# The residual kept in the output tensors, and the last sum made by accumulating DMAs: one layer of a retention / convolution / expert model on one core

## Chip, cores and metric
The kernel runs on one core of a Trainium2 chip. The metric is the device time of one execution in microseconds (us); lower is better. Everything is computed in fp32.

## The reference, cut to what matters
One layer is applied to 128 context tokens (x_prompt) and 1024 latent tokens (x_sample), width 1024. For each group of tokens:

```python
h = rmsnorm(x, n_pre_mix) * (1.0 + sc1) + sh1
m, s_f, s_b = mixer(h, ...)                 # retention and short convolution, then @ w_o
x = x + g1 * rmsnorm(m, n_post_mix)         # the residual, called x1 below
h = rmsnorm(x, n_pre_ffn) * (1.0 + sc2) + sh2
f = expert_choice_ffn(h, ...)               # 16 experts, each takes its best 128 + 16 tokens
x = x + g2 * rmsnorm(f, n_post_ffn)         # the output
```

`rmsnorm(f, g)` is `f * rsqrt(mean(f*f) + 1e-6) * g`. The expert outputs of one token, from however many experts chose it, are summed into f. The outputs are the new x of both groups and the two final retention states of the context.

## The kernel before, in words
The 1152 tokens are nine tiles of 128 rows: tile 0 is the context, tiles 1 to 8 are the latent tokens. The program gives each engine its own list of instructions; semaphores order them. Nothing is scheduled by a tool: what stands first in an engine's list is issued first, and a wait holds all that stands behind it on that engine.

- **Up to about 1290 us**: modulation, input projection, retention and convolution, with TensorE on weights that are split in a high and a low part (L743 to L745).
- **Mixing, about 1290 to 1410 us**: for each tile, TensorE multiplies by w_o. DVE makes x1 from the product, the gate and the tile of x (L1674, L1679), and then the experts' input h2 (L1687, L1689). ACT squares and sums for the two norms (L1226, L1232). POOL turns each sum into a reciprocal root by `rstd` (L580 to L584: an add, a wait for it, a pow), and stores x1 (L633) and h2 (L638) to the scratch tensors x1_d and h2_d in DRAM. `store(t, b)` does this for tile t and buffer b; it runs in a loop of four passes with two tiles each, and once more for tile 8 (L640 to L643).
- **Routing, to about 1480 us**: the experts' tokens are chosen; ffn_d, the sum of the expert outputs in DRAM, is filled with zeros by nine stores of POOL (L650).
- **Experts, to 2298 us**: for each of 16 experts POOL gathers its rows of h2 by an indirect DMA, TensorE multiplies by the three weights (L976), DVE scales the result (L1797, L1799), and POOL adds its 128 and 16 rows into ffn_d by two indirect accumulating DMAs (L673, L675). SP loads the weights. Once the fifth unit of the last expert is made, SP also loads all nine tiles of x1 from x1_d to x1_all (L559).
- **The last part**, which the change rewrites. SP waits until all rows are added, then loads f in three groups of three tiles (f_all, L563). ACT squares and sums the nine tiles in order (L1303, `f_sq`). For each group, POOL multiplies the third tile by g2 (already holding the gate times n_post_ffn; L683), then makes `rstd` of the group's three sums (L582, L584). DVE multiplies the first two tiles by g2 (L1810), waits for the group's `rstd`, and computes y = (f * g2) * rstd + x1 for three tiles (L1816). SP stores each tile of y to the outputs as it becomes ready (L567), and waits for all stores.

Queues: DMAs issued by SP and ACT go through the hardware queue (q1 in the profile), those of POOL through the software queue (q0). All use the same 16 DMA engines.

The tail of DVE before:

```python
for g in range(3):
    dve.wait_ge(f_in_s[g], 16)
    for t in (3 * g, 3 * g + 1):
        did(dve.tensor_tensor(y_all[:, t, :], f_all[:, t, :], g2[:, min(t, 1), :], ALU.mult))
    settle()
    dve.wait_ge(f_rstd, g + 1)
    for t in range(3 * g, 3 * g + 3):
        if t % 3 == 2:
            dve.wait_ge(f_scaled, g + 1)
        dve.scalar_tensor_tensor(y_all[:, t, :], y_all[:, t, :], f_rs[:, t:t + 1], x1_all[:, t, :], ALU.mult, ALU.add)
```

Of the kernel before, what the change touches and what calls it, by code (L numbers as in the profile page):

```python
# [6 lines left out]
ALU = mybir.AluOpType  # L7
# [6 lines left out]
P = 128  # L14
D = 1024
# [3 lines left out]
NT = TOK // P  # L19
# [5 lines left out]
EXPERTS = 16  # L25
# [100 lines left out]
class Steps:  # L126
# [5 lines left out]
    def did(self, ins):  # L132
        ins.then_inc(self.sem, 1)
        self.n += 1

    def settle(self):
        self.eng.wait_ge(self.sem, self.base + self.n)
# [23 lines left out]
def build(nc, x_prompt, x_sample, state_f, state_b, c, c_ctx, w_ada, b_ada, n_pre_mix, n_post_mix,  # L161
          n_pre_ffn, n_post_ffn, w_in, dec_f, dec_b, gn_g, conv_w, w_ret_o, w_conv_o, w_o, w_router,
          w_gate, w_up, w_down, small_tab, rope_tab, y_prompt, y_sample, new_f, new_b):
    with ExitStack() as ctx:
        BASE = 16512

        def at(name, offset, shape, dt=F32):
            return nc.alloc_sbuf_tensor_at(name, shape, dt, offset=BASE + offset)

        def sem(name):  # L170
            return ctx.enter_context(nc.semaphore(name))

        def dram(name, shape):
            return nc.dram_tensor(name, shape, F32, kind="Internal").ap()
# [49 lines left out]
        f_ms, f_rs = x_ms, x_rstd  # L224
# [58 lines left out]
        x1 = [at(f"x1_{j}", Z + (14 + j) * SL, [P, D]) for j in range(2)]  # L283
# [32 lines left out]
        g2 = at("g2", Z + 9 * SL, [P, 2, D])  # L316
        norm_ffn = at("norm_ffn", Z + 17 * SL, [P, D])
        sq3 = at("sq3", Z + 16 * SL, [P, D])
        x1_all = at("x1_all", 0, [P, NT, D])
        f_all = at("f_all", 10 * SL, [P, NT, D])  # L320
        y_all = at("y_all", Z, [P, NT, D])

# [8 lines left out]

        mod_d = dram("mod_d", [2, 4 * D])
        merged_d = dram("merged_d", [KD, P, TOK])
        x1_d = dram("x1_d", [NT, P, D])
        h2_d = dram("h2_d", [TOK, D])
        ffn_d = dram("ffn_d", [TOK, D])

# [52 lines left out]
        xg_turned, xT_ready, out_turned, out_ready = sem("xg_turned"), sem("xT_ready"), sem("out_turned"), sem("out_ready")  # L390
        added_l, added_c = sem("added_l"), sem("added_c")
        g2_in = sem("g2_in")
        x1_landed = sem("x1_landed")
        f_in_s = [sem(f"f_in_s{g}") for g in range(3)]
        f_sq, f_rstd, f_scaled = sem("f_sq"), sem("f_rstd"), sem("f_scaled")
        y_ready, y_stored = sem("y_ready"), sem("y_stored")
        m_rstd, x1_rstd, gn_var, gn_rstd = sem("m_rstd"), sem("x1_rstd"), sem("gn_var"), sem("gn_rstd")

        tally = {}
# [14 lines left out]
        def _(sp):  # L414
# [140 lines left out]
                    load_unit(e, j, False)  # L555


            sp.wait_ge(unit_made, 12 * (EXPERTS - 1) + 5)
            sp.dma_start(x1_all[:], x1_d.rearrange("t p d -> p t d")).then_inc(x1_landed, 16)  # L559
            sp.wait_ge(added_l, 16 * EXPERTS)  # L560
            sp.wait_ge(added_c, 16 * EXPERTS)
            for g in range(3):
                sp.dma_start(f_all[:, 3 * g:3 * g + 3, :], ffn_d[3 * g * P:(3 * g + 3) * P, :].rearrange("(t p) d -> p t d", p=P))\  # L563
                  .then_inc(f_in_s[g], 16)
            for t in range(NT):
                sp.wait_ge(y_ready, t + 1)
                sp.dma_start(ys[t - 1] if t else yp, y_all[:, t, :]).then_inc(y_stored, 16)  # L567
            sp.wait_ge(y_stored, 16 * NT)


        @block.gpsimd
        def _(pool):
# [7 lines left out]
            def rstd(dst, src, eps):  # L580

                pool_steps.did(pool.tensor_tensor(dst, src, eps, ALU.add))  # L582
                pool_steps.settle()
                return pool.tensor_tensor(dst, dst, minus_half[:, 0:dst.shape[-1]], ALU.pow)  # L584
# [40 lines left out]
                pool.dma_start(merged_d[n], merged[:]).then_inc(merged_stored, 16)  # L625


            def store(t, b):
                pool.wait_ge(m_sq, t + 1)
                rstd(stats[:, 8 + b:9 + b], stats[:, 4 + b:5 + b], rms_eps[:, 0:1]).then_inc(m_rstd, 1)  # L630
                pool.wait_ge(x1_ready, t + 1)
                plain(pool)
                pool.dma_start(x1_d[bass.ds(t, 1)].rearrange("a p d -> (a p) d"), x1[b][:]).then_inc(x1_stored[b], 16)  # L633
                pool.wait_ge(x1_sq, t + 1)
                rstd(stats[:, 12 + b:13 + b], stats[:, 6 + b:7 + b], rms_eps[:, 0:1]).then_inc(x1_rstd, 1)
                pool.wait_ge(h2_ready, t + 1)
                plain(pool)
                pool.dma_start(h2_d[bass.ds(t * P, P), :], h2[b][:]).then_inc(h2_stored[b], 16)  # L638

            with pool_steps.loop(4, 4) as i:  # L640
                store(2 * i, 0)
                store(2 * i + 1, 1)
            store(8, 0)  # L643

            pool.wait_ge(logit_made, NT)
# [30 lines left out]
                                        compute_op=ALU.add).then_inc(added_c, 16)  # L676


            pool.wait_ge(g2_ready, 2)
            for g in range(3):  # L680
                ts, t = slice(3 * g, 3 * g + 3), 3 * g + 2
                pool.wait_ge(f_in_s[g], 16)
                pool.tensor_tensor(y_all[:, t, :], f_all[:, t, :], g2[:, 1, :], ALU.mult).then_inc(f_scaled, 1)  # L683
                pool.wait_ge(f_sq, 3 * g + 3)
                rstd(f_rs[:, ts], f_ms[:, ts], rms_eps[:, ts]).then_inc(f_rstd, 1)
            pool.wait_ge(state_stored, 32 * HEADS)


# [618 lines left out]
        def _(dve):  # L1307
# [495 lines left out]


            dve.wait_ge(g2_ready, 2)
            dve.wait_ge(x1_landed, 16)
            for g in range(3):
                dve.wait_ge(f_in_s[g], 16)
                for t in (3 * g, 3 * g + 1):
                    did(dve.tensor_tensor(y_all[:, t, :], f_all[:, t, :], g2[:, min(t, 1), :], ALU.mult))  # L1810
                settle()
                dve.wait_ge(f_rstd, g + 1)
                for t in range(3 * g, 3 * g + 3):
                    if t % 3 == 2:
                        dve.wait_ge(f_scaled, g + 1)
                    dve.scalar_tensor_tensor(y_all[:, t, :], y_all[:, t, :], f_rs[:, t:t + 1], x1_all[:, t, :], ALU.mult, ALU.add)\  # L1816
                       .then_inc(y_ready, 1)


# [26 lines left out]
```

## Time and profile before

| what | value |
|---|---|
| median of three runs | 2342.23 us (2341.36 to 2344.58) |
| span of the profiled execution, first to last instruction | 2342.5 us |
| granted TensorE clock, mean | 0.965 of full speed (2.4 GHz) |
| busy: PE / PEld / DVE / ACT / POOL | 2148.6 / 2036.2 / 707.5 / 372.5 / 183.2 us |
| DMA | 357.37 MB, mean 153 GB/s |
| end of the last transposes on PE | 2297.7 us |
| last operation on DVE starts | 2338.0 us |

The profiled execution is known by its span of 2342.54 us, the first instruction's start to the last one's end; it is 0.3 us over the median of the runs.

How to read it: PE is TensorE's matmuls, PEld its weight loads, DVE VectorE, ACT ScalarE, POOL GpSimd, SP the engine that only issues DMAs. L12 is line 12 of the kernel; a helper's line is named for all that it issues. Buffer numbers and digits are left out of names, so x_d is x1_d, x_all is x1_all, h_d is h2_d. Times are us from the start of the span. In a line of the timeline the columns are start, duration, engine, line, operation, output<-inputs with shapes, count, and in brackets the idle time ahead of it with what ended it. A DMA line with "GB/s" gives the rate in 40 equal slices of its window; under it each queue has its packets, MB and the time of its packets as a share of 16 engines' window.

### The profile page before, as it was taken

The page shows a single profiled execution, that of the slowest core. Times are in us where ns is not written, and L with a number is a line of the kernel's source. Part 1 is how long each engine was busy: PE and PEld are TensorE (multiplying, and loading weights), DVE is VectorE, ACT ScalarE, POOL GpSimd, SP SyncE. Part 2 cuts the span into 40 slices and gives each one's busy share as a digit, 9 for nine tenths or more (in the row PEclk, how much of TensorE's full clock was granted, in tenths as well). Part 3 has the DMA queues.
Part 4 walks back from the last instruction along what each step waited for, and adds up shares of the span by engine and source line. Part 5 has one row for each costly group of instructions (what it writes and reads, how often), then busy time and mean ns, then how long its engine had stood idle before and what let it go on. Part 6 is the DMA issues. An engine that isn't in the chain of part 4 may idle for free.

```text
span 2342.5 us, 34417 instructions
## 1 busy us (share of the span) xinstructions
PE 2148.6 (92%) x14065; PEld 2036.2 (87%) x14065; DVE 707.5 (30%) x1203; ACT 372.5 (16%) x586; POOL 183.2 (8%) x245
## 2 busy tenths in 40 slices
PE   5899999997999999999999892899999999999992
PEld 1689898987999999999999781899999999999992
DVE  1634343446655323232123547001000000100004
ACT  4421212122111121111112330100000000000001
POOL 1000000000000000000000211001100000110003
PEclk9999999999999999999999995899999999999996
DMA  8101010101444211112225638588888888888854
GB/s 280 29 27 38 20 37 19 37 19 55 134 142 137 81 45 36 52 37 75 85 76 201 216 127 305 191 269 254 273 277 277 270 262 268 253 272 279 277 197 172
DMA packets 329939, 357.37 MB, mean 153 GB/s; under 512 B 9924, under 2 KB 297612, under 8 KB 329764
## 3 DMA queue, kind: packets, MB, share of 16 engines
q1 hardware_dynamic: 315760, 308.41, 41.5%
q0 software_dynamic: 14032, 48.29, 6.9%
q8 instruction: 32, 0.52, 0.1%
q14 instruction: 15, 0.12, 0.0%
q10 hardware_dynamic: 100, 0.03, 0.0%
HBM read 318.39 MB, written 38.31 MB: 152 GB/s over the span
## 4 chain that ended last, share of the span: by engine, by line
PE 85%; issue 5%; DVE 5%; DMA 2%; ACT 1%; POOL 1%; ACTq 0%; DVEq 0%; SPq 0%; POOLq 0%
PE ps L976 32%; PE ps L743 13%; PE ps L745 13%; PE ps L744 13%; PE ps L900 1%; PE ps L902 1%; PE ps L901 1%; PE ps L778 1%; DMA xa<-in_x_sample_dram 1%; PE ps L1004 1%; PE ps L917 1%; PE ps L792 1%; PE ps L784 1%; PE ps L966 1%; PE ps L1006 1%
## 5 line engine op out<-in xcount | busy, mean ns | idle before, releaser
L743 PE MATMUL ps<-h_hi,w_hi 128*128 128x384 f32 x1536 | 524.2, 341 | 10.9 <-DVE h_lo L1372 8.7
L744 PE MATMUL ps<-h_lo,w_hi 128*128 128x384 f32 x1536 | 515.6, 336 | 0.0
L745 PE MATMUL ps<-h_hi,w_lo 128*128 128x384 f32 x1536 | 515.3, 336 | 0.0
L976 PE MATMUL ps<-xT,wq 128*128 128x144 f32 x4096 | 506.3, 287 | 1.3 <-ACT xT L1276 1.3
L976 PEld LDWEIGHTS ps<-xT,wq 128*128 128x128 f32 x4096 | 504.5, 191 | 1.7 <-ACT xT L1276 1.4
L743 PEld LDWEIGHTS ps<-h_hi,w_hi 128*128 128x128 f32 x1536 | 290.2, 189 | 25.2 <-issue 12.5
L744 PEld LDWEIGHTS ps<-h_lo,w_hi 128*128 128x128 f32 x1536 | 290.2, 189 | 1.9 <-issue 1.9
L745 PEld LDWEIGHTS ps<-h_hi,w_lo 128*128 128x128 f32 x1536 | 289.9, 189 | 0.0
L976 PE MATMUL ps<-hid,wq 128*128 128x144 f32 x2048 | 255.1, 287 | 0.7 <-issue 0.7
L976 PEld LDWEIGHTS ps<-hid,wq 128*128 128x128 f32 x2048 | 251.7, 190 | 1.3 <-issue 0.9
L1378 DVE TENSOR_TENSOR w_lo<-w_raw,w_hi 128x1024 fp32r<-128x1024 f32 x80 | 97.6, 1220 | 227.2 <-ACT w_hi L1063 226.6
L1791 DVE TENSOR_TENSOR hid<-ps,sg 128x288 f32<-128x288 f32 x64 | 29.3, 458 | 450.5 <-PE ps L976 450.5
L743 PE MATMUL ps<-z_hi,w_hi 128*128 128x384 f32 x384 | 128.5, 335 | 0.0
L745 PE MATMUL ps<-z_hi,w_lo 128*128 128x384 f32 x384 | 128.4, 334 | 0.0
L744 PE MATMUL ps<-z_lo,w_hi 128*128 128x384 f32 x384 | 128.4, 334 | 0.0
L1797 DVE TENSOR_SCALAR ot_l<-ps,val_l 128x1024 f32<-128x1024 f32 x16 | 20.5, 1284 | 312.4 <-PE ps L1006 312.4
L1063 ACT CAST w_hi<-w_raw 128x1024 fp32r<-128x1024 f32 x80 | 83.9, 1049 | 160.6 <-PE ps L745 86.1
L1285 ACT ACTIVATE sg<-ps 128x288 f32<-128x288 f32 x64 | 26.2, 410 | 453.2 <-PE ps L976 453.2
L1563 DVE SCALAR_TENSOR_TENSOR ada_acc<-ada_k,cond,ada_acc 128x512 f32<-128x512 f32 x112 | 79.2, 749 | 41.6 <-DMA ada_k<-in_w_ada_dram 40.2
L673 POOL DMA_INDIRECT ffn_d<-ot_l,idx_l x16 | 25.8, 1612 | 738.9 <-DVE ot_c L1799 738.9
L743 PEld LDWEIGHTS ps<-z_hi,w_hi 128*128 128x128 f32 x384 | 72.1, 188 | 0.2 <-issue 0.2
L744 PEld LDWEIGHTS ps<-z_lo,w_hi 128*128 128x128 f32 x384 | 72.1, 188 | 0.0
(227 smaller groups left out, 1786.1 us busy)
## 6 DMA issues: line engine op xcount, KB each, us to landing
wq<-in_w_down_dram SPq DMA_DIRECT2D x64, 1024.0 KB, 5.4
wq<-in_w_gate_dram SPq DMA_DIRECT2D x64, 1024.0 KB, 7.1
wq<-in_w_up_dram SPq DMA_DIRECT2D x64, 1024.0 KB, 7.1
w_raw<-in_w_in_dram SPq DMA_DIRECT2D x64, 512.0 KB, 4.1
ada_k<-in_w_ada_dram SPq DMA_DIRECT2D x64, 256.0 KB, 2.8
merged_d<-merged POOLq DMA_DIRECT2D x16, 576.0 KB, 3.5
ada<-in_w_ada_dram SPq DMA_DIRECT2D x4, 2048.0 KB, 14.4
ret_part<-merged_d POOLq DMA_DIRECT2D x8, 576.0 KB, 4.2
```

The source lines that it names most:

```text
L673: pool.indirect_dma_start(ffn_d, bass.IndirectOffsetOnAxis(ap=idx_l[:, e:e + 1], axis=0), ot_l[:], None, compute_op=ALU.add).then_inc(adde ...
L743: pe.matmul(out, w_hi[:, slot, k, :], xh, start=(k == 0), stop=False)
L744: pe.matmul(out, w_hi[:, slot, k, :], xl, start=False, stop=False)
L745: mm = pe.matmul(out, w_lo[:, slot, k, :], xh, start=False, stop=(k == KD - 1))
L778: return pe.matmul(bank(b, 512), lhsT, src[:, 1 + 4 * x:5 + 4 * x, :], start=True, stop=True)
L784: mm = pe.transpose(ps[:, b, s * P:(s + 1) * P], src[:, t, :], ident)
L976: mm = pe.matmul(ps[:, j % 4, m * CAP:(m + 1) * CAP], wq[j][:, k, m * P:(m + 1) * P], src[:, k, :], start=(k == 0), stop=(k == KD - 1))
L1063: act.copy(w_hi[:, c_ % 2], w_raw[:, c_ % 2]).then_inc(w_hi_done, 1)
L1285: act.activation(sg[:], unit_of(2 * q), ACT.Silu).then_inc(unit_act, 1)
L1378: dve.tensor_tensor(w_lo[:, c_ % 2], w_raw[:, c_ % 2], w_hi[:, c_ % 2].bitcast(F32), ALU.subtract)\
L1563: ins = dve.scalar_tensor_tensor(ada_acc[:, w_, :], ada_k[k % 2][:], cond[:, k, w_:w_ + 1], ada_acc[:, w_, :], ALU.mult, ALU.add)
L1791: dve.tensor_tensor(hid[:, 2 * q:2 * q + 2, :], ps[:, (2 * q + 1) % 4, 0:2 * CAP].rearrange("p (m n) -> p m n", m=2), sg[:], ALU.mult)\
```

## The change
x1 is no longer stored to a scratch tensor: POOL's stores in the mixing part write it straight to the outputs (tile 0 to y_prompt, the others to y_sample), and it is not read back. In the last part DVE makes one operation for each tile, y_all = (f * rstd) * g2, and POOL issues an accumulating DMA for each tile that adds y_all to the x1 that lies in the output. The multiplies on POOL and the first multiplies on DVE go. POOL's order in the last part is: rstd 1, rstd 2, adds of group 1, rstd 3, adds of group 2, adds of group 3. POOL's store loop has its first pass written out ahead of the loop, since tile 0 goes to another tensor. The whole diff:

```diff
@@ -316,7 +316,6 @@
         g2 = at("g2", Z + 9 * SL, [P, 2, D])
         norm_ffn = at("norm_ffn", Z + 17 * SL, [P, D])
         sq3 = at("sq3", Z + 16 * SL, [P, D])
-        x1_all = at("x1_all", 0, [P, NT, D])
         f_all = at("f_all", 10 * SL, [P, NT, D])
         y_all = at("y_all", Z, [P, NT, D])
 
@@ -331,7 +330,6 @@
 
         mod_d = dram("mod_d", [2, 4 * D])
         merged_d = dram("merged_d", [KD, P, TOK])
-        x1_d = dram("x1_d", [NT, P, D])
         h2_d = dram("h2_d", [TOK, D])
         ffn_d = dram("ffn_d", [TOK, D])
 
@@ -390,10 +388,9 @@
         xg_turned, xT_ready, out_turned, out_ready = sem("xg_turned"), sem("xT_ready"), sem("out_turned"), sem("out_ready")
         added_l, added_c = sem("added_l"), sem("added_c")
         g2_in = sem("g2_in")
-        x1_landed = sem("x1_landed")
         f_in_s = [sem(f"f_in_s{g}") for g in range(3)]
-        f_sq, f_rstd, f_scaled = sem("f_sq"), sem("f_rstd"), sem("f_scaled")
-        y_ready, y_stored = sem("y_ready"), sem("y_stored")
+        f_sq, f_rstd = sem("f_sq"), sem("f_rstd")
+        y_ready, y_added = sem("y_ready"), sem("y_added")
         m_rstd, x1_rstd, gn_var, gn_rstd = sem("m_rstd"), sem("x1_rstd"), sem("gn_var"), sem("gn_rstd")
 
         tally = {}
@@ -555,17 +552,12 @@
                     load_unit(e, j, False)
 
 
-            sp.wait_ge(unit_made, 12 * (EXPERTS - 1) + 5)
-            sp.dma_start(x1_all[:], x1_d.rearrange("t p d -> p t d")).then_inc(x1_landed, 16)
             sp.wait_ge(added_l, 16 * EXPERTS)
             sp.wait_ge(added_c, 16 * EXPERTS)
             for g in range(3):
                 sp.dma_start(f_all[:, 3 * g:3 * g + 3, :], ffn_d[3 * g * P:(3 * g + 3) * P, :].rearrange("(t p) d -> p t d", p=P))\
                   .then_inc(f_in_s[g], 16)
-            for t in range(NT):
-                sp.wait_ge(y_ready, t + 1)
-                sp.dma_start(ys[t - 1] if t else yp, y_all[:, t, :]).then_inc(y_stored, 16)
-            sp.wait_ge(y_stored, 16 * NT)
+            sp.wait_ge(y_added, 16 * NT)
 
 
         @block.gpsimd
@@ -625,21 +617,29 @@
                 pool.dma_start(merged_d[n], merged[:]).then_inc(merged_stored, 16)
 
 
+            def add_to_output(g):
+                for t in range(3 * g, 3 * g + 3):
+                    pool.wait_ge(y_ready, t + 1)
+                    pool.dma_start(ys[t - 1] if t else yp, y_all[:, t, :], accum_op=ALU.add).then_inc(y_added, 16)
+
             def store(t, b):
+
                 pool.wait_ge(m_sq, t + 1)
                 rstd(stats[:, 8 + b:9 + b], stats[:, 4 + b:5 + b], rms_eps[:, 0:1]).then_inc(m_rstd, 1)
                 pool.wait_ge(x1_ready, t + 1)
                 plain(pool)
-                pool.dma_start(x1_d[bass.ds(t, 1)].rearrange("a p d -> (a p) d"), x1[b][:]).then_inc(x1_stored[b], 16)
+                dst = yp if isinstance(t, int) and t == 0 else ys[bass.ds(t - 1, 1)].rearrange("a p d -> (a p) d")
+                pool.dma_start(dst, x1[b][:]).then_inc(x1_stored[b], 16)
                 pool.wait_ge(x1_sq, t + 1)
                 rstd(stats[:, 12 + b:13 + b], stats[:, 6 + b:7 + b], rms_eps[:, 0:1]).then_inc(x1_rstd, 1)
                 pool.wait_ge(h2_ready, t + 1)
                 plain(pool)
                 pool.dma_start(h2_d[bass.ds(t * P, P), :], h2[b][:]).then_inc(h2_stored[b], 16)
 
-            with pool_steps.loop(4, 4) as i:
+            def two_stores(i):
                 store(2 * i, 0)
                 store(2 * i + 1, 1)
+            pool_steps.each(4, 4, two_stores)
             store(8, 0)
 
             pool.wait_ge(logit_made, NT)
@@ -676,13 +676,13 @@
                                         compute_op=ALU.add).then_inc(added_c, 16)
 
 
-            pool.wait_ge(g2_ready, 2)
             for g in range(3):
-                ts, t = slice(3 * g, 3 * g + 3), 3 * g + 2
-                pool.wait_ge(f_in_s[g], 16)
-                pool.tensor_tensor(y_all[:, t, :], f_all[:, t, :], g2[:, 1, :], ALU.mult).then_inc(f_scaled, 1)
+                ts = slice(3 * g, 3 * g + 3)
                 pool.wait_ge(f_sq, 3 * g + 3)
                 rstd(f_rs[:, ts], f_ms[:, ts], rms_eps[:, ts]).then_inc(f_rstd, 1)
+                if g:
+                    add_to_output(g - 1)
+            add_to_output(2)
             pool.wait_ge(state_stored, 32 * HEADS)
 
 
@@ -1803,18 +1803,10 @@
 
 
             dve.wait_ge(g2_ready, 2)
-            dve.wait_ge(x1_landed, 16)
-            for g in range(3):
-                dve.wait_ge(f_in_s[g], 16)
-                for t in (3 * g, 3 * g + 1):
-                    did(dve.tensor_tensor(y_all[:, t, :], f_all[:, t, :], g2[:, min(t, 1), :], ALU.mult))
-                settle()
-                dve.wait_ge(f_rstd, g + 1)
-                for t in range(3 * g, 3 * g + 3):
-                    if t % 3 == 2:
-                        dve.wait_ge(f_scaled, g + 1)
-                    dve.scalar_tensor_tensor(y_all[:, t, :], y_all[:, t, :], f_rs[:, t:t + 1], x1_all[:, t, :], ALU.mult, ALU.add)\
-                       .then_inc(y_ready, 1)
+            for t in range(NT):
+                dve.wait_ge(f_rstd, t // 3 + 1)
+                dve.scalar_tensor_tensor(y_all[:, t, :], f_all[:, t, :], f_rs[:, t:t + 1], g2[:, min(t, 1), :], ALU.mult, ALU.mult)\
+                   .then_inc(y_ready, 1)
 
 
 # ---- launch: one core; inputs and outputs as the reference has them ----
```

## Rows read from the trace of the kernel before
**Rows 1.** The page, part 4: the chain that ended last, by engine.
```profile
PE 85%; issue 5%; DVE 5%; DMA 2%; ACT 1%; POOL 1%; ACTq 0%; DVEq 0%; SPq 0%; POOLq 0%
```

**Rows 2.** Busy time by stretch (columns: us; PE, PEld, DVE, ACT, POOL busy; PEclk, DMA share, GB/s).
```profile
1560.00:2290.00 730.00, 721.43 (x5923) 713.43 (x5922) 60.58 (x85) 62.57 (x142) 65.96 (x54) 1.00 0.84 261
...
2290.00:2345.00 55.00, 7.21 (x59) 6.57 (x58) 26.70 (x17) 11.14 (x20) 18.95 (x11) 0.62 0.51 182
```

**Rows 3.** Chain that ended last, in order of time, from 2290 us.
```profile
2302.63 4.65 DMA ffn_d<-ot_c,idx_c
...
2307.35 6.38 DMA f_all<-ffn_d
...
2319.52 5.26 DVE y_all L1816 x3
...
2325.12 4.50 DVE y_all L1810 x2
...
2335.63 1.28 DVE y_all L1816
```

**Rows 4.** Timeline of ACT and POOL in the last part.
```profile
2317.47 0.96 POOL L582 TENSOR_TENSOR stats<-stats,small 128x3 f32<-128x3 f32 x1 [0.17 <-ACT sq L1303]
...
2318.51 0.89 POOL L584 TENSOR_TENSOR stats<-stats,small 128x3 f32<-128x3 f32 x1
...
2321.21 0.19 ACT L1303 ACTIVATION_READ_ACCUMULATOR sq<-f_all 128x1 f32 x1
...
2321.69 1.17 POOL L582 TENSOR_TENSOR stats<-stats,small 128x3 f32<-128x3 f32 x1
...
2322.95 1.77 POOL L584 TENSOR_TENSOR stats<-stats,small 128x3 f32<-128x3 f32 x1
...
2324.93 0.19 ACT L1303 ACTIVATION_READ_ACCUMULATOR sq<-f_all 128x1 f32 x1
```

**Rows 5.** Instructions on the tile y_all (min/median/max ns, first and last start).
```profile
L1816 DVE SCALAR_TENSOR_TENSOR y_all<-y_all,stats,x_all x9: 1271/1280/3289, 2319.5 to 2338.0; 128x1024 f32<-128x1024 f32 x9
...
L567 SPq DMA_DIRECT2D out_dram<-y_all x9: 332/332/356, 2322.8 to 2339.3; - x9
```

**Rows 6.** Traffic of the last scatter-add: 2302 to 2307, 2304.5 to 2306, 2305 to 2305.5, 2300 to 2308.
```profile
GB/s 0 0 0 0 0 0 0 426 98 0 0 66 131 33 98 66 229 66 131 197 229 131 229 164 229 229 197 229 164 229 262 164 164 230 164 66 98 0 0 0
...
q0 software_dynamic: 77, 0.31, 102.8%
...
2305.00:2305.50 0.50, 0.00 (x0) 0.00 (x0) 0.00 (x0) 0.00 (x0) 0.00 (x0) 0.50 1.11 221
...
q0 software_dynamic: 176, 0.59, 48.0%
```

**Rows 7.** The two operations of `rstd` elsewhere (tiles stats and gnr, whole span).
```profile
L582 POOL TENSOR_TENSOR stats<-stats,small x22: 179/194/1176, 41.4 to 2327.4; 128x1 f32<-128x1 f32 x18, 128x3 f32<-128x3 f32 x3, 128x9 f32<-128x9 f32 x1
...
L584 POOL TENSOR_TENSOR gnr<-gnr,small x24: 565/1007/1024, 160.8 to 548.5; 128x4 f32<-128x4 f32 x16, 128x1 f32<-128x1 f32 x8
```

**Rows 8.** POOL's DMA issues: timeline, traffic from 1395.5 to 1401.5, tile ffn_d.
```profile
1290.69 1.45 POOL L584 TENSOR_TENSOR stats<-stats,small 128x1 f32<-128x1 f32 x1
...
1396.17 0.60 POOL L633 DMA_DIRECT2D x_d<-x  x1 [3.61 <-DVE x L1679]
...
GB/s 0 0 0 0 0 0 0 0 0 0 109 0 328 410 355 410 410 355 410 410 273 28 27 27 27 27 0 0 0 0 0 0 0 0 0 0 0 0 0 0
...
x_d<-x POOLq DMA_DIRECT2D x1, 512.0 KB, 3.8
...
1423.78 0.53 POOL L650 DMA_DIRECT2D ffn_d<-zero  x1 [0.37 <-issue]
...
L673 POOL DMA_INDIRECT ffn_d<-ot_l,idx_l x16: 1589/1611/1630, 1532.8 to 2300.7; - x16
```

**Rows 9.** Traffic from 2322.5 to 2345 us, in 40 slices.
```profile
GB/s 0 0 379 415 393 408 386 422 393 0 0 0 0 0 0 0 218 415 386 408 408 408 415 138 0 0 0 357 415 386 415 401 408 408 7 0 0 0 0 0
```

**Rows 10.** Busy time while x1 is read back, same columns as rows 2.
```profile
2269.00:2279.00 10.00, 9.64 (x79) 9.43 (x77) 0.69 (x2) 0.41 (x1) 0.00 (x0) 1.00 1.02 409
```

## The prediction
> **What bounds the kernel now.** The chain that ended last comes first: TensorE carries 85% of the span [rows 1]. Busy time by stretch then shows that the change lies almost wholly outside that part. In the expert stage (1560 to 2290 us) PE is busy 721 of 730 us, while in the last 55 us it has 7 us of work and what the other engines and the DMA do is the span [rows 2]. The chain in order of time gives the links of that end: the last scatter-add lands at 2307.28, the first third of f_all at 2313.73, and from 2319.52 the chain is DVE alone, alternating between L1816 and L1810 until the last y tile [rows 3]. The last store is issued at 2339.3 [rows 5], and the span ends at 2342.54. The traffic from 2322.5 on shows three bursts of about 400 GB/s with empty slices between them, so now the stores wait for DVE and not DVE for the stores [rows 9]. ACT is not late: its ninth square is done at 2325.12, 14 us before the last store [rows 4].
>
> **Removed from the path.** DVE loses six multiplies (the two on the chain at 2325.12 cost 4.50 us) and POOL its three, which shared the time with DVE: L1816 takes 1.28 us in the median and 3.29 at worst [rows 3, 5]. What is left for DVE is nine operations of 1.28 us, 11.5 us instead of the 19.8 from 2319.52 to 2339.3. Read alone, this promises some 8 us. It is not the forecast, because the transfers change kind.
>
> **Added: nine adds to DRAM.** No direct accumulating DMA is in this trace; the nearest rows are the scatter-add of expert 15, 144 rows of 4 KB from SBUF added into DRAM, which ran with no other traffic. From 2304.5 to 2306, in its steady part, 77 packets passed with the 16 queues busy to 102.8%: 16 x 1.5 / 77 = 0.312 us for a 4 KB packet on one DMA engine, 205 GB/s [rows 6]. A plain store or load runs at 400 to 415 GB/s [rows 8, 9], so an added row costs twice a stored one. The change adds 9 x 128 = 1152 rows, 72 for each of the 16 engines: 72 x 0.312 = **22.4 us**. One end of the bound is the best half microsecond, 221 GB/s [rows 6]: 4.72 MB / 221 = 21.4 us. A lower end is the plain rate, 408 GB/s [rows 9]: 11.6 us. The upper end is the mean packet of the whole scatter-add, its slow start included: 48.0% of 16 x 8 us over 144 packets is 0.427 us [rows 6], and 72 of them take 30.7 us. I take 0.312, since 1152 packets in a row are much nearer to the steady part than to the start; the direct form has the same 4 KB rows and adds in the same DMA engines.
>
> The start costs extra once. All 144 rows, 9 for an engine, went from 2302.87 to about 2306.6 [rows 6], 3.7 us where 9 x 0.312 is 2.8: **0.9 us**.
>
> **When the stream can begin.** The third square ends at 2317.4 and POOL starts `rstd` at 2317.47 as now [rows 4]. Its first operation took 0.96 us beside DVE's multiply; with DVE idle such an operation takes 0.18 to 0.19 [rows 4, 7]. The second took 0.89 with DVE mostly idle, between the 0.57 and 1.01 of one and four columns elsewhere [rows 4, 7]. So rstd 1 is done at 2317.47 + 0.20 + 0.08 + 0.89 = 2318.65, not 2319.40. DVE makes y 0 to 2 from 2318.75 to 2318.75 + 3 x 1.28 = 2322.6. The sixth square is done at 2321.40 [rows 4]. POOL's add then runs beside DVE (1.17 us as now), to 2322.6, and its pow mostly without it (0.89): rstd 2 at 2323.6. Bounds: 0.2 for the first gives 2322.6, and 1.77 for the second, as now, 2324.5 [rows 4]. Only after rstd 2 does POOL come to the first add, although y 0 has been ready since 2320.0: three ready tiles stand behind a wait for a later group's squares. A direct store on POOL shows its first bytes 0.83 us after its start (1396.17, traffic from 1397.0) [rows 8]. First packet: 2323.65 + 0.83 = **2324.5**.
>
> **Can POOL and DVE feed it?** One direct issue takes 0.53 us and comes every 0.90 [rows 8]; even at the 1.61 + 0.30 us of a scatter-add [rows 8] it is below the 8 x 0.312 = 2.50 us that one tile's add occupies the DMA engines. Tiles 3 to 5 are ready by 2327.5 (DVE from 2323.7), when the first three adds run until 2332.9. rstd 3 stands behind the three issues, 2323.65 + 3 x 0.90 = 2326.35, and is done by 2327.5 to 2329.4; y 8 by 2333.3 at worst, when the queue still holds adds until 2347. The queue never runs empty, so DVE's 8 us and every delay of rstd 3 cost and give nothing.
>
> **The sum.** 2324.5 + 0.9 + 22.4 = 2347.8 for the last byte. What follows the last byte is read from the end of the span before: the traffic stops at about 2341.65, the start of its last slice with a trace of it [rows 9], and the span ends 0.9 us later, landing and SP's last wait included; the scatter-add's last byte came 0.7 us ahead of its landing [rows 3, 6], which gives no other size. 2347.8 + 0.9 = 2348.7, against the span of 2342.54 +6.2. The median of the three runs is 2342.23, 0.3 below that span, so the forecast is **2348.4 us**.
>
> **Edits at nothing.** The x1 stores go to the outputs instead of a scratch tensor: same queue, place, bytes. The read of x1_all goes (4.6 MB at 409 GB/s), one issue on SP: PE was busy 9.64 of 10 us meanwhile [rows 10], so it covers the load, and at most 0.4 us comes back; SP has nothing else to issue until the last scatter-add lands at 2307.28 [rows 3]. The peeled first pass of POOL's loop: code met for the first time cost at most 1.45 - 0.57 = 0.9 us at 1290.69 [rows 7, 8], and a second copy of the body could cost that again, where `rstd` holds DVE. The removed waits for g2 on POOL and x1 on DVE were long fulfilled. I carry these as -0.4 to +0.9.
>
> **Rules weighed.** Traffic to DRAM reaches 415 GB/s here [rows 9], in both directions of this last part. The Trainium skill, DMA: Bandwidth & Descriptors, section Specifications, gives one core some 358 GB/s of HBM; an add both reads and writes its destination there, 9.4 MB, which by an estimate from that figure takes 26.4 us and ends the kernel at 2352.4. The trace does not agree for plain traffic, and its add moves 2 x 205 GB/s there.
>
> **Rivals.** (a) *The add runs at the plain rate*, the half rate of the scatter-add being due to its indirect rows. Then the stream is 11.6 us: 2324.5 + 11.6 + 0.9 = 2337.0. The producers allow about as much: rstd 3 at 2327.5 to 2329.4, three tiles of DVE more (y 8 at 2331.4 to 2333.3), then 0.83 + 1.3 (0.52 MB at 408 GB/s) + 0.9, 2336.3 at worst. As a time **2336.7**, faster than before. The point from which it decides: the time of before is kept where 72 packets take 2342.54 - 2324.5 - 1.8 = 16.2 us, 0.23 us for each; below that the change gains. For it: all accumulating rows of this trace are indirect. Against: their rate is steady across the burst and half the plain one, as if each row were read twice. The Trainium skill, DMA: Bandwidth & Descriptors, section Anatomy of one DMA, fits a POOL-issued DMA as 2.0 us plus its bytes over 436 GB/s, with no surcharge for adding; by it the stream would be 10.8 us, which is this rival. The 205 GB/s measured speak against it [rows 6].
> (b) *Plain rate, but POOL pays for an accumulating issue as for a scatter-add*, 1.61 + 0.30 us: nine issues and one `rstd` in a row, 2323.65 + 17.2 + 1.2 = 2342.0, then 0.3 + 1.3 + 0.9: 2344.5, as a time **2344.2**, within the bound of no change. For it: POOL would be the only engine that still works. Against: the direct stores' 0.53 us [rows 8].
> (c) *The adds don't overlap*: each pays the start again, 0.9 + 2.5 = 3.4 us, nine take 30.6 instead of 23.3: **2355.7**. The mean packet above gives nearly the same (30.7). Against: the three stores of a group run without a gap [rows 9], though those come from the other queue.
>
> **How the numbers follow.** A measurement of this kernel can tell about 0.2% from no change, 4.7 us: over 2346.9 is slower, under 2337.5 faster. The forecast's case has 0.77, the others 0.10 (a), 0.05 (b) and 0.08 (c). Within the forecast's case the earliest start (-1.0), the best rate (-1.0), a start cost of nothing (-0.9) and x1_all's 0.4 reach 2345.1; I give 0.15 to its part under 2346.9 and 0.62 above. So slower 0.70, same 0.20, faster 0.10. The range leaves out (a) and half of (b): 2344.5 to 2356.0.
>
> **What would show it.** In the profile after: first bytes of the last traffic near 2324.5; then one unbroken stretch at about 205 GB/s for 22 to 23 us, not three bursts; POOL's nine issues done by about 2334; DVE's nine operations at 1.28 us each, over by 2333; the chain's last link a DMA into the output. The prediction is wrong if that traffic passes 300 GB/s, if it has gaps (then the feeding, not the rate, is the bound), or if PE's last matmul ends over 1 us away from 2297.7, since that would be an effect of the edits ahead of the last part.

## The result, and the profile after

The changed kernel takes **2355.04 us** in the median of four runs (2353.13 to 2356.89), the kernel before 2343.29 in its four (2341.36 to 2344.58): slower by 0.51%, ratio 1.0051 with a 95% interval of 1.0036 to 1.0065. The forecast was 2348.4 with a range to 2356.0: the sign is right and the value inside, but the forecast had only 6.2 of the 11.75 us.

The page of the changed kernel, its first part and its queues:

```profile
span 2355.2 us, 34387 instructions
...
PE 2149.1 (91%) x14065; PEld 2036.6 (86%) x14065; DVE 694.5 (29%) x1197; ACT 372.5 (16%) x586; POOL 178.5 (8%) x251
...
q1 hardware_dynamic: 313296, 298.97, 40.2%
q0 software_dynamic: 15328, 53.01, 7.9%
```

PE did the same work in the same time. The 4.7 MB that q1 wrote as y now pass through q0 (53.01 MB, not 48.29), and q1 has lost another 4.7 MB, x1's way back. The loss is not ahead of the last part: PE's last transposes start at 2297.06, 0.4 us later than before, and in the other kernels below, with the same work up to there, they start between 2294.4 and 2297.2.

The timeline of the last part, POOL and DVE of the changed kernel (beside [rows 4, 5]):

```profile
2317.82 0.19 POOL L574 TENSOR_TENSOR stats<-stats,small 128x3 f32<-128x3 f32 x1 [13.47 <-ACT sq L1303]
2318.09 0.89 POOL L576 TENSOR_TENSOR stats<-stats,small 128x3 f32<-128x3 f32 x1
...
2319.10 3.68 DVE L1808 SCALAR_TENSOR_TENSOR y_all<-f_all,stats,g 128x1024 f32<-128x1024 f32 x3 [18.25 <-POOL stats L576]
...
2321.83 1.00 POOL L574 TENSOR_TENSOR stats<-stats,small 128x3 f32<-128x3 f32 x1 [2.85 <-ACT sq L1303]
...
2322.91 0.86 POOL L576 TENSOR_TENSOR stats<-stats,small 128x3 f32<-128x3 f32 x1
...
2323.72 2.75 POOL L623 DMA_DIRECT2D out_dram<-y_all  x3
2323.80 3.68 DVE L1808 SCALAR_TENSOR_TENSOR y_all<-f_all,stats,g 128x1024 f32<-128x1024 f32 x3 [1.02 <-POOL stats L576]
...
2325.63 1.88 POOL L574 TENSOR_TENSOR stats<-stats,small 128x3 f32<-128x3 f32 x1
2327.60 0.88 POOL L576 TENSOR_TENSOR stats<-stats,small 128x3 f32<-128x3 f32 x1
2328.45 5.25 POOL L623 DMA_DIRECT2D out_dram<-y_all  x6
2328.51 3.68 DVE L1808 SCALAR_TENSOR_TENSOR y_all<-f_all,stats,g 128x1024 f32<-128x1024 f32 x3 [1.04 <-POOL stats L576]
```

DVE makes its nine operations in three groups of 3.68 us and is done at 2332.2; before, it was done at 2339.3. The first add is issued at 2323.72, six issues in a row end at 2333.70. Then no instruction computes for 21 us. What happens in them is seen in the traffic from 2322 to 2352, in 40 slices of 0.75 us:

```profile
GB/s 0 0 0 0 87 126 208 180 202 169 202 197 197 213 218 202 213 213 197 208 218 202 213 213 208 213 213 218 202 202 218 213 213 208 208 87 11 0 0 0
...
q0 software_dynamic: 1296, 4.72, 82.9%
```

This is one unbroken stream from the slice at 2325.0 to about 2349.5, at 205 GB/s in the mean from 2326 to 2348 (slices of 197 to 218), where before there were three bursts of 400 [rows 9]. The packets took 82.9% of 16 x 30 us; over 1152 rows of 4 KB that is 0.345 us a row. And the traffic ends almost 6 us ahead of the span. The queue of SP's waits and the instructions that close the program (line, engine's sequencer, operation: duration in ns, start) tell what lies there:

```profile
SPq L164 <- DMA out_dram<-y_all: 40.9, 1, 40.9
SPq L164 <- PEq L164: 4.8, 1, 4.8
```

```profile
L164 POOLq EVENT_SEMAPHORE  x2: 17/17/17, 2355.0 to 2355.1; - x2
...
L164 POOLq COMPARE_BRANCH  x1: 41/41/41, 2332.7 to 2332.7; - x1
L164 POOLq DRAIN  x1: 22086/22086/22086, 2332.9 to 2332.9; - x1
L164 SPq COMPARE_BRANCH  x1: 38/38/38, 2350.2 to 2350.2; - x1
```

SP has its last landing at 2350.2 and then waits 4.8 us more (the name PEq is that of an engine in the closing meeting, not of the late one). The late one is POOL: behind its last instruction stands a DRAIN, which holds until 2355.0. In the trace of before, DVE's DRAIN ends with DVE's last operation, at 2339.3, and ACT's with ACT's, at 2325.1; POOL's does not. A DRAIN is taken up while the operation ahead of it still runs, so its end is what counts here, not its own duration. POOL's last operation and the same two lines in the kernel before:

```profile
2328.61 1.71 POOL L584 TENSOR_TENSOR stats<-stats,small 128x3 f32<-128x3 f32 x1
...
L164 POOLq DRAIN  x1: 11718/11718/11718, 2328.7 to 2328.7; - x1
...
L164 SPq COMPARE_BRANCH  x1: 38/38/38, 2342.2 to 2342.2; - x1
```

There the DRAIN ended at 2340.4, 10.1 us behind POOL's last operation (2328.61 + 1.71 = 2330.32) and 33 us behind the last landing of a DMA of POOL, and DVE's work hid it by 2 us. It is in no busy time and on no chain of the page.

### The profile page after: what moved, and what is told of

The parts are those of the page before. It is cut to its first block, busy times and chain, and to the rows that moved or that the text cites. A ratio compares the mean times of both kernels' runs of the same rounds, so it can differ in the third digit from the quotient of the medians.

```text
span 2355.2 us, 34387 instructions
## 1 busy us (share of the span) xinstructions
PE 2149.1 (91%) x14065; PEld 2036.6 (86%) x14065; DVE 694.5 (29%) x1197; ACT 372.5 (16%) x586; POOL 178.5 (8%) x251
## 3 DMA queue, kind: packets, MB, share of 16 engines
q0 software_dynamic: 15328, 53.01, 7.9%
## 4 chain that ended last, share of the span: by engine, by line
PE 84%; issue 5%; DVE 4%; DMA 2%; POOL 1%; ACT 1%; ACTq 0%; DVEq 0%; SPq 0%; POOLq 0%
PE ps L976 32%; PE ps L743 13%; PE ps L745 13%; PE ps L744 13%; PE ps L900 1%; PE ps L902 1%; PE ps L901 1%; PE ps L778 1%; DMA xa<-in_x_sample_dram 1%; PE ps L1004 1%; PE ps L917 1%; PE ps L792 1%; PE ps L784 1%; PE ps L966 1%; PE ps L1006 1%
## 5 line engine op out<-in xcount | busy, mean ns | idle before, releaser
L745 PEld LDWEIGHTS ps<-z_hi,w_lo 128*128 128x128 f32 x384 | 72.1, 188 | 0.0
```

The source lines that it names most:

```text
L745: mm = pe.matmul(out, w_lo[:, slot, k, :], xh, start=False, stop=(k == KD - 1))
```

## The experiments

Theory A at their start is in two parts: an adding row costs twice a plain one, which is a property of adding, not of POOL's queue (the software queue, q0); and POOL's closing DRAIN takes some 10 us from POOL's last work, of which the last 4.8 us come only after its last DMA has landed. Each time stands beside runs of the kernel before on the same chip; "end" is the end of the profiled span, and SP's COMPARE_BRANCH in the lines below marks the last landing that SP waits for.

### Plain stores from POOL's queue

```diff
-pool.dma_start(ys[t - 1] if t else yp, y_all[:, t, :], accum_op=ALU.add).then_inc(y_added, 16)
+pool.dma_start(ys[t - 1] if t else yp, y_all[:, t, :]).then_inc(y_added, 16)
```

> The changed kernel with the accumulation taken out of the nine last DMAs, which now overwrite the output: the addition of x1 is left out. Same queue, same issuing engine, same bytes written. Theory A (the adding doubles the time of a packet on the DMA engines, and POOL's closing DRAIN ends some 4.8 us after the last landing): packets of about 0.16 us, so the last traffic is bound by the producers and ends near 2335 to 2338, at about 400 GB/s in bursts; the span ends 4.8 us after the last landing or 10 us after POOL's last issue, about 2343 to 2345, some 11 us under the changed kernel. Rival B (the software queue, not the adding, sets the half rate): the stream stays at about 205 GB/s and the span near 2355.

Measured: 2344.07 us, ratio 1.0002 (0.9992 to 1.0011). The traffic of that run from 2320 to 2360, its last issue and its closing:

```profile
GB/s 422 123 0 0 0 344 336 406 393 274 344 385 401 393 397 393 397 254 0 0 0 0 0 0 0 0 0 0 0 0 0 0 0 0 0 0 0 0 0 0
...
q0 software_dynamic: 1296, 4.72, 30.3%
```

```profile
2332.44 0.53 POOL L623 DMA_DIRECT2D out_dram<-y_all  x1 [0.67 <-DVE y_all L1808]
```

```profile
L164 POOLq DRAIN  x1: 10357/10357/10357, 2332.6 to 2332.6; - x1
L164 SPq COMPARE_BRANCH  x1: 38/38/38, 2338.2 to 2338.2; - x1
```

The same 1296 packets through the same queue take 30.3% of 16 x 40 us, 0.168 us for each row of 4 KB, at up to 400 GB/s. So **adding doubles the row, the queue does not**. The second reading matters as much: even with the rows at the plain rate the kernel is no faster than before. DVE is done at 2332.1, the last row lands at 2338.2, but the last issue of POOL ends at 2332.97 and its DRAIN at 2343.0, 10.0 us later. That is also 4.8 us behind the last landing, so this run alone doesn't tell which of the two parts of A held the DRAIN.

### POOL waits for the adds

```diff
             pool.wait_ge(state_stored, 32 * HEADS)
+            pool.wait_ge(y_added, 16 * NT)
```

> The changed kernel, where POOL also waits for all nine adds before its list ends, so that its closing DRAIN starts only after the last landing at about 2350.2. Theory A (the DRAIN has a length of its own, about 10 us from POOL's last work, and runs beside the adds; in the changed kernel it is then held by the open DMAs): it now starts at 2350.2 and the span ends near 2360, 5 us later. Theory B (the DRAIN is only held by open software-queue DMAs and ends 4.8 us after the last landing whenever it starts): the span stays within 1 us of 2355. Theory C (with nothing open it returns at once): the span ends near 2351, 4 us earlier.

Measured: 2358.02 us (2357.56 to 2360.09), ratio 1.0066 (1.0049 to 1.0083), 3.0 us over the changed kernel's median.

```profile
L164 SPq COMPARE_BRANCH  x1: 38/38/38, 2346.5 to 2346.5; - x1
...
L164 POOLq DRAIN  x1: 8929/8929/8929, 2346.7 to 2346.7; - x1
```

With nothing open the DRAIN takes 8.9 us by itself. Theory B wanted the end 4.8 us behind the last landing, theory C right behind it. The profiled span, 2355.9, would by itself fit B, but PE's last transposes start 2.6 us earlier in this execution, and the closing lines put the end 9.1 us behind the landing. A holds; its 10 us were 1 too many here, and the extra time was 3.0 instead of 5 us, since the adds were also in about 1 us sooner, counted from the last scatter-add. In the changed kernel only 4.8 us lie behind the landing, so some 4 us of the DRAIN's time seem to run beside the adds.

### POOL waits for the stores in the kernel before

```diff
             pool.wait_ge(state_stored, 32 * HEADS)
+            pool.wait_ge(y_stored, 16 * NT)
```

> The kernel before, where POOL also waits for the nine stores of y (issued by SP) before its list ends. No DMA of POOL is open in this part, the last landed at 2307.3. Theory A (the DRAIN has about 10 us of its own, which the kernel before hides behind DVE's work): it starts near 2342.2 and the span ends at about 2352, 10 us over before. Theory B (the DRAIN follows only open software-queue DMAs): it ends at once and the span stays at 2342.5.

Measured: 2352.75 us, ratio 1.0041 (1.0026 to 1.0055), 9.7 us over the kernel before.

```profile
L164 SPq COMPARE_BRANCH  x1: 38/38/38, 2340.6 to 2340.6; - x1
...
L164 POOLq DRAIN  x1: 10113/10113/10113, 2340.8 to 2340.8; - x1
```

One wait that costs nothing by itself makes the kernel before nearly as slow as the changed one. No DMA of POOL was open. The DRAIN is 10.1 us long and counts from POOL's last instruction, here a wait.

### x1 in the outputs, and nothing else

```diff
-pool.dma_start(x1_d[bass.ds(t, 1)].rearrange("a p d -> (a p) d"), x1[b][:]).then_inc(x1_stored[b], 16)
+dst = yp if isinstance(t, int) and t == 0 else ys[bass.ds(t - 1, 1)].rearrange("a p d -> (a p) d")
+pool.dma_start(dst, x1[b][:]).then_inc(x1_stored[b], 16)
...
-sp.dma_start(x1_all[:], x1_d.rearrange("t p d -> p t d")).then_inc(x1_landed, 16)
+sp.dma_start(x1_all[:, 0, :], yp).then_inc(x1_landed, 16)
+sp.dma_start(x1_all[:, 1:NT, :], ys.rearrange("t p d -> p t d")).then_inc(x1_landed, 16)
```

The first pass of POOL's store loop is written out too, as in the change.

> One part of the change alone on the kernel before: x1 is stored straight into the outputs (with the first pass of the loop written out), is read back from there, and the last part stays as before. Theory A (this part costs nothing): within 1 us of before, the last transposes on PE end within 0.5 us of 2297.7. Rival (storing into the outputs or the longer code of POOL costs something): 1 to 3 us more, visible already in the mixing stage, 1290 to 1410 us.

Measured: 2341.72 us, ratio 0.9997 (0.9987 to 1.0006): no difference, as expected of the time. PE's last transposes start at 2294.97 and end 1.7 us earlier than in the profile of before; the expected 0.5 us was too narrow, since this point moves by 2.8 us from kernel to kernel (2294.4 to 2297.2), and nothing got later. So these edits cost nothing that can be measured, and all of the loss is in the last part.

### The adds ahead of the next rstd

```diff
                 rstd(f_rs[:, ts], f_ms[:, ts], rms_eps[:, ts]).then_inc(f_rstd, 1)
-                if g:
-                    add_to_output(g - 1)
-            add_to_output(2)
+                add_to_output(g)
```

> The changed kernel with POOL's order in the last part turned: the adds of a group stand right behind its rstd, ahead of the next rstd. Theory A (the end is the stream of adds plus a fixed 4.8 us of DRAIN behind the last landing): the first add is issued at about 2320.5 instead of 2323.7, the stream of 22.5 us and the end move up by the same 3 us, span near 2352, though rstd 2 and 3 and DVE come later. Rival (POOL's last issue decides, which moves only if DVE does): the last issue stays near 2333 and the span within 1 us of 2355.

Measured: 2352.42 us (2349.11 to 2353.92), ratio 1.0039 (1.0024 to 1.0055), 2.6 us under the changed kernel's median.

```profile
2318.64 0.98 POOL L623 DMA_DIRECT2D out_dram<-y_all  x1 [1.71 <-DVE y_all L1806]
...
2333.57 0.86 POOL L623 DMA_DIRECT2D out_dram<-y_all  x1 [0.56 <-DVE y_all L1806]
```

```profile
L164 POOLq DRAIN  x1: 17002/17002/17002, 2333.7 to 2333.7; - x1
L164 SPq COMPARE_BRANCH  x1: 38/38/38, 2345.9 to 2345.9; - x1
```

The last issue is no earlier than in the changed kernel, though f's load was 2.2 us earlier; the first one is 5.1 us earlier, 2.9 us beyond that shift. The last landing (2345.9) is 4.3 us earlier, 2.1 beyond the shift, and the end once more lies 4.8 us behind it (2350.8). The rival, that the last issue decides, falls: POOL's last issue ends at 2334.4, 16 us ahead of the end. It is the stream that sets the end, plus 4.8 us. Theory A had put 3 us on it and 2.6 were measured in the medians, though the ranges of the two kernels touch (2353.13 is the changed kernel's lowest).

### DVE's saving alone

```diff
-                if g:
-                    add_to_output(g - 1)
-            add_to_output(2)
...
+            for t in range(NT):
+                sp.wait_ge(y_ready, t + 1)
+                sp.dma_start(ys[t - 1] if t else yp, y_all[:, t, :]).then_inc(y_added, 16)
             sp.wait_ge(y_added, 16 * NT)
```

> DVE's saving alone: the changed kernel, where SP stores the nine tiles of y with plain DMAs (the addition of x1 is left out) and POOL ends with rstd 3. Theory A (POOL's DRAIN takes 10 us from its last work): DVE is done at 2332.2 and the last store would be in by 2335.3, but POOL's last work ends near 2327.5 to 2328.5 and the DRAIN at about 2338: span near 2338, 4 to 5 us under before, where the one-operation tile alone would give 7. Rival (the DRAIN costs nothing if no DMA of POOL is open): span near 2335.5, 7 us under before. Against the plain stores issued by POOL (span 2343.2) it tells what moving the last issue to POOL costs: 5 us.

Measured: 2338.69 us, ratio 0.9985 (0.9975 to 0.9994).

```profile
2326.08 1.77 POOL L579 TENSOR_TENSOR stats<-stats,small 128x3 f32<-128x3 f32 x1
```

```profile
L164 POOLq DRAIN  x1: 11780/11780/11780, 2326.2 to 2326.2; - x1
...
L164 SPq COMPARE_BRANCH  x1: 38/38/38, 2334.4 to 2334.4; - x1
```

SP has all landings at 2334.4, and the end waits for POOL's DRAIN, until 2338.0, 10.1 us behind its last pow (2327.85). DVE is done at 2331.6 instead of 2339.3, but this is worth less than four us in the medians even when nothing is paid for it, because before the change the DRAIN ended only 2 us ahead of the span. The difference to the run with plain stores from POOL (ratio 1.0002, span 2343.2) is the price of issuing the last DMAs from POOL: 4.0 us by the ratios, 5.0 by the spans, of which 0.5 are PE's later end there.

### POOL's multiplies given to DVE

```diff
-pool.tensor_tensor(y_all[:, t, :], f_all[:, t, :], g2[:, 1, :], ALU.mult).then_inc(f_scaled, 1)
...
-for t in (3 * g, 3 * g + 1):
+for t in range(3 * g, 3 * g + 3):
     did(dve.tensor_tensor(y_all[:, t, :], f_all[:, t, :], g2[:, min(t, 1), :], ALU.mult))
...
+times_g2(0); times_g2(1); plus_x1(0); times_g2(2); plus_x1(1); plus_x1(2)
```

> The kernel before with one thing changed in the last part: POOL's three multiplies go to DVE, which makes 18 operations instead of 15, ordered so that it never waits for an rstd. Theory A (each multiply of POOL slowed DVE's operations beside it by about 2 us, more than the 1.2 us that it saved): DVE runs 18 operations of 1.21 to 1.28 us without a gap from 2313.9 to about 2336.2, the last store lands at 2339, span near 2339.5, 3 us under before; POOL's last work ends near 2327.5, its DRAIN near 2337.5, still hidden. Rival (DVE's slow operations are slow for another reason): DVE ends near 2340 to 2342 and the kernel is 1 to 2 us slower than before.

Measured: 2340.56 us, ratio 0.9991 (0.9982 to 1.0000), just under what can be told from no change. The tile y_all and the closing:

```profile
L1807 DVE TENSOR_TENSOR y_all<-f_all,g x9: 1215/1218/1224, 2313.6 to 2326.7; 128x1024 f32<-128x1024 f32 x9
L1812 DVE SCALAR_TENSOR_TENSOR y_all<-y_all,stats,x_all x9: 1276/1277/1284, 2320.8 to 2333.9; 128x1024 f32<-128x1024 f32 x9
```

```profile
2325.00 2.92 POOL L582 TENSOR_TENSOR stats<-stats,small 128x3 f32<-128x3 f32 x1 [1.02 <-ACT sq L1300]
...
2328.00 1.89 POOL L584 TENSOR_TENSOR stats<-stats,small 128x3 f32<-128x3 f32 x1
```

```profile
L164 POOLq DRAIN  x1: 11900/11900/11900, 2328.1 to 2328.1; - x1
...
L164 SPq COMPARE_BRANCH  x1: 37/37/37, 2338.3 to 2338.3; - x1
```

DVE's part of A is right: 18 operations, none over 1.28 us (before, up to 3.29 [rows 5]), done at 2335.2 instead of 2339.3 although there are three more. The new order of DVE's list is part of the gain: before, DVE stood idle for 1.14 us in front of the first L1816, waiting for rstd 1. But the rest of A slipped: beside DVE's dense work POOL's two tiny operations took 2.92 and 1.89 us, its last work ended at 2329.9, and the DRAIN at 2340.0 set the end, 1.7 us behind SP.

### Loads of one tile, on the kernel above

```diff
-for g in range(3):
-    sp.dma_start(f_all[:, 3 * g:3 * g + 3, :], ffn_d[3 * g * P:(3 * g + 3) * P, :].rearrange("(t p) d -> p t d", p=P)).then_inc(f_in_s[g], 16)
+for t in range(NT):
+    sp.dma_start(f_all[:, t, :], ffn_d[t * P:(t + 1) * P, :]).then_inc(f_in_s[t], 16)
```

ACT and DVE wait for each tile's own semaphore; all else is the kernel with DVE's multiplies.

> The kernel of the run before this one, and f is loaded by nine DMAs of one tile instead of three of three tiles, so that the squares and multiplies can begin with the first tile. Theory A: the first tile lands near 2310.5 instead of 2313.7, all work of DVE and ACT moves up by 3.2 us, DVE ends near 2333, POOL's last work near 2325 and its DRAIN near 2335: span near 2336, 6 us under before, a difference that can be measured. Rival (the loads of one tile come at a lower rate, so that DVE waits between tiles; or the DRAIN of POOL, 10 us behind its last work, sets the end): span 2337 to 2339.

Measured: 2338.56 us, ratio 0.9983 (0.9974 to 0.9992). The first square starts 3.97 us behind the first issue of a load (2306.50 to 2310.47) instead of 6.4. DVE's first six multiplies take 7.49 us where they took 3.49 and 3.50 with loads of three tiles, so the loads hold DVE by only 0.5 us. The end is again POOL's:

```profile
L164 POOLq DRAIN  x1: 11905/11905/11905, 2325.3 to 2325.3; - x1
...
L164 SPq COMPARE_BRANCH  x1: 38/38/38, 2335.5 to 2335.5; - x1
```

A's 2336 was missed for the reason that the rival named: the DRAIN ends at 2337.2, SP was done at 2335.5.

### One operation of POOL for each group, on the kernel above

```diff
-rstd(f_rs[:, ts], f_ms[:, ts], rms_eps[:, ts]).then_inc(f_rstd, 1)
+pool.tensor_tensor(f_rs[:, ts], f_rs[:, ts], minus_half[:, ts], ALU.pow).then_inc(f_rstd, 1)
...
+dve.tensor_scalar(f_rs[:, ts], f_ms[:, ts], RMS_EPS, None, ALU.add).then_inc(f_eps, 1)
```

DVE makes the sum with eps of group 1 behind its fourth multiply, that of group 2 behind its first sum with x1, that of group 3 behind its seventh multiply, each ahead of work that does not need it.

> The kernel with loads of one tile, where the sum with eps of each rstd goes from POOL to a small operation of DVE, so that POOL makes one pow for each group and its last work ends earlier; DVE's nine and nine large operations stay. Theory A (the end of that kernel is POOL's last work plus 10.2 us of DRAIN, 2327.1 + 10.2 = 2337.3, while SP had its last landing at 2335.5): POOL's last pow ends near 2325, its DRAIN near 2335.2, and the end falls back to SP's last landing plus the 0.3 us or so of closing, span near 2336.2, 1.2 us less, though DVE gets three operations more. Rival (the end follows the stores, and the DRAIN only happens to lie there): span 2337.5 or a little more, since DVE has more to do.

Measured: **2337.13 us**, ratio 0.9974 (0.9965 to 0.9983) to the kernel before.

```profile
2321.92 0.16 DVE L1806 TENSOR_SCALAR stats<-stats 128x3 f32<-128x3 f32 x1
...
2322.16 2.89 POOL L681 TENSOR_TENSOR stats<-stats,small 128x3 f32<-128x3 f32 x1 [1.78 <-DVE stats L1806]
2324.38 7.26 DVE L1816 SCALAR_TENSOR_TENSOR y_all<-y_all,stats,x_all 128x1024 f32<-128x1024 f32 x6
```

```profile
L164 POOLq DRAIN  x1: 12900/12900/12900, 2322.3 to 2322.3; - x1
...
L164 SPq COMPARE_BRANCH  x1: 38/38/38, 2334.8 to 2334.8; - x1
```

POOL's last pow ends at 2325.05, its DRAIN at 2335.2; SP is done at 2334.8, so the two ends now lie 0.4 us apart, the DRAIN's still the later one. The span fell by 2.1 us, of which 0.9 are PE's earlier end; the 1.2 left are what A said. This version, which keeps x1_d and the plain stores, beats the kernel before by 0.26% and the changed one by 0.76% in the medians.

## Why the prediction was right, and where it was short

**Right: the stream is the bound.** The step that added rows take 0.312 us came out at 0.345 over the whole stream, the start cost in it. 22.4 + 0.9 = 23.3 us were forecast, 24.4 measured. Some 0.6 us of the difference were in the prediction's own rows: of its 77 packets two were under 512 bytes, and the engines were busy to 102.8%, so that 0.312 us stands for 210 GB/s while the traffic was 205; at 205 GB/s the 4.72 MB take 23.0 us, and 205 is what the flat part showed. The stream began at 2325.0 (forecast 2324.5). The first add was issued when it was forecast, though PE was 0.4 us late, but its first bytes came 1.5 us behind the issue (2325.2, in slices of 0.1 us) and not 0.83. The stream ended near 2349.4. The lower end, 11.6 us at the plain rate, is near what POOL's plain stores take (72 x 0.168 = 12.1), while the rows of the indirect scatter-add were the right stand-in for the direct add.

The two rules weighed, both from the Trainium skill, DMA: Bandwidth & Descriptors, did not give the stream. By the fit with 436 GB/s for a DMA of POOL (section Anatomy of one DMA) it was an estimated 10.8 us; the adds took 24.4. By the 358 GB/s of HBM for one core (section Specifications) it was an estimated 26.4 us, 2 too long.

**Right: what feeds it.** rstd 1 was done at 2318.98 (2318.65 forecast, +0.4 for PE's end), the first add issued at 2323.72 (2323.65), DVE done at 2332.2, POOL at 2333.7 (by about 2334). An adding issue took 0.86 us on POOL, not the 0.53 of a plain one nor the 1.61 of a scatter-add, which changed nothing since a tile's stream is 2.5 us. Once flowing, the stream had no gap.

**Right: edits at nothing.** Storing x1 in the outputs alone gave 0.9997.

**What the change consists of.** Three runs give its steps, by their ratios to the kernel before: the shorter work of DVE alone 0.9985, with the stores issued by POOL 1.0002, with the adding 1.0051. That is about -3.5, +4.0 and +11.5 us. The prediction had a price for the third only, and took the first as hidden.

**Short: the term behind the last byte.** The sum set 0.9 us from the last byte to the end, read from the end of before, where the last DMA was SP's. Measured: 5.8 us. That one term is 4.9 of the 6.5 us by which the span (2355.2) went past the sum (2348.7); the stream is 1.1 of it and its later start 0.5. The step failed because the change moves the last work of the program from SP to POOL, and a row that the chain of the page does not show, POOL's DRAIN of 10.1 us, was taken for nothing. It could have been read before: the closing instructions stood in the trace, with a DRAIN that ended 2.1 us ahead of the span. The sign that the chain's last link would be a DMA into the output did not come either: the chain of the page ends with POOL's issues, since neither the stream nor the DRAIN is on it.

**Luck in the range.** That 2355.04 still lay inside is partly luck. The upper end, 2356.0, was set just over rival (c), adds that don't overlap (2355.7), which did not happen; by chance it left room for a term that the prediction did not have. The sign needed no luck: without the 4.9 us the kernel would still be some 7 us slower.

**Short: rival (a).** It said 2336.7 for adds at the plain rate. The run with plain stores from POOL measured that case, but for the adding: 2344.07. Its last landing, 2338.2, is 1.2 us behind the end that the rival's sum gave (2337.0); the other 5 us are the DRAIN, which after a last issue at 2333 ended at 2343. So the change did not win even at the plain rate, and the 0.10 given to "faster" rested on an end without the DRAIN. Rival (b), a dearer issue, also left the DRAIN out. Rival (c), adds that don't overlap, fell by the unbroken stream.

**A step that held by chance: from span to time.** The sum took the time as the span less 0.3 us. Each profiled execution whose time is listed is 1.7 us longer by its time than by its span (2356.89 beside 2355.2), so the profiled execution of before lay some 2 us over the median, and the two differences nearly cancel. In the changed kernel the profiled execution was again the slowest, 1.85 us over its median, and they cancel again (2354.9 by the span, 2355.04 measured). Had a faster execution been profiled, spans and medians would not have been comparable to better than 2 us.

## What to carry to other kernels

An accumulating DMA is not a free addition: here its rows took twice the transfer time of stored ones (0.345 against 0.168 us), so put it beside work, not behind it. Before the last instruction of a program is moved to another engine, read the closing instructions of each engine in the trace; here whatever POOL does last must end 10 us ahead of everything else, or it sets the end. And work given to POOL to help DVE can cost more than it saves when the two run side by side: with its three large multiplies taken from POOL, DVE was done 3.8 us sooner (2335.2 against 2339.3, f's load 0.3 earlier), with three operations more; at most 1.1 us of this is the new order.

## What the runs showed of the hardware that was not expected

- POOL's closing DRAIN takes 8.9 to 10.1 us with no DMA of POOL open (10.1 in the kernel before, with SP's plain stores, with POOL waiting for SP's stores, and in the last three kernels; 8.9 where POOL waited for its own adds). With adds open it ends 4.8 us behind their last landing, in the changed kernel (2350.2 to 2355.0) and with the adds early (2345.9 to 2350.8). With plain stores of POOL open it ended 10.0 us behind the last issue and 4.8 behind the last landing. This fits a first half that runs beside the open DMAs and a second half that waits for them; that it is built so was not tried, nor why 8.9 and not 10.1.
- Adding 4 KB rows in DRAM ran at 205 GB/s in the flat part, 0.32 us a row for each of 16 DMA engines (0.345 by the packets' time over the whole stream); storing the same rows through the same queue took 0.168 us. Direct adds (205 GB/s over 22 us) and the indirect ones of the last scatter-add (205 GB/s over 1.5 us) cost the same.
- POOL's add and pow on 128x3 elements take 0.19 and 0.89 us with DVE idle, and up to 3.16 and 1.90 us beside DVE's 128x1024 operations with two inputs in SBUF (in the run with loads of one tile):

```profile
2321.94 3.16 POOL L581 TENSOR_TENSOR stats<-stats,small 128x3 f32<-128x3 f32 x1 [0.78 <-ACT sq L1299]
...
2325.18 1.90 POOL L583 TENSOR_TENSOR stats<-stats,small 128x3 f32<-128x3 f32 x1
```

- DVE was held in turn only by POOL's large multiplies: beside POOL's tiny operations it never took over 1.28 us. The Trainium skill, SBUF — State Buffer, section Who interferes with whom, says that a DVE instruction with two SBUF inputs contends with a GpSimd instruction that reads SBUF. The trace agrees: with the multiplies gone from POOL, L1812 takes 1.28 us at most, before up to 3.29.
